# Two chained transformer layers: the decay levels, the memory keys and the hand-over between the layers reordered

## The reference, cut to what matters

```python
# first layer
xn   = rms_norm(x, norm1_g)
proj = xn @ w_in                                   # hq hf hi hgate gq gk gv glow ggate
o    = concat(hgrn2_mixer(...), gla_mixer(...))    # causal, decayed scores; per-head norm, silu gate
h    = x + o @ w_out
h    = h + peer_ffn(rms_norm(h, norm2_g), w_q, sub_keys, u, v)
x1   = rms_norm(h, norm_f_g)
# second layer
cols   = rms_norm(x1, norm_pre_2) @ w_in_2         # four branches and 4 x 1024 gate logits
mem_kv = rms_norm(mem_2, norm_mem_2) @ w_mem_kv_2  # memory keys (512 columns), values (512)
merged = sum_n sigmoid(gates[n]) * (ys[n] @ w_up_2[n])
out    = x1 + rms_norm(merged @ w_out_2, norm_post_2)
```

## Time and profile before

| | us |
|---|---|
| median of 3 runs | 1450.87 (1449.73 to 1451.43) |
| profiled execution, time | 1450.22 |
| profiled execution, span of its trace | 1448.4 |

### The profile page before, as it was taken

How to read it: one execution, slowest core, us unless ns; L and a number is a source line. 1 busy time by engine, 2 the same in 40 slices (tenths; PEclk the granted TensorE clock), 3 DMA queues, 4 the chain that set the end, 5 groups by cost and what they waited for, 6 DMA issues and landing times.

```text
span 1448.4 us, 22172 instructions
## 1 busy us (share of the span) xinstructions
PE 1415.0 (98%) x7922; PEld 1220.9 (84%) x7922; DVE 989.8 (68%) x1739; ACT 736.5 (51%) x1115; POOL 184.5 (13%) x176
## 2 busy tenths in 40 slices
PE   8998999999999999999999999999999999999998
PEld 8877888698788888888888888888889899888786
DVE  6577469899766666666666666666668564665565
ACT  5644321277555555555555555555555734465343
POOL 0062124699100000000000000000010100000000
PEclk9999999999999999999999999999999999999999
DMA  5442542211465555555555555555544432434442
GB/s 200 178 154 86 179 143 87 101 49 42 150 199 188 188 188 188 188 189 188 189 188 191 188 189 188 191 187 192 180 145 170 154 138 95 146 117 160 176 159 102
DMA packets 56342, 229.14 MB, mean 158 GB/s; under 512 B 6736, under 2 KB 7008, under 8 KB 47456
## 3 DMA queue, kind: packets, MB, share of 16 engines
q1 hardware_dynamic: 55824, 228.19, 46.4%
q10 hardware_dynamic: 464, 0.20, 0.0%
HBM read 226.27 MB, written 2.10 MB: 158 GB/s over the span
## 4 chain that ended last, share of the span: by engine, by line
PE 85%; DVE 7%; ACT 3%; DMA 2%; issue 1%; POOL 1%; ACTq 0%; DVEq 0%; POOLq 0%
PE ps L2265 22%; PE ps L2055 15%; PE ps L2254 13%; PE ps L2021 9%; PE ps L2252 8%; PE ps L2240 4%; PE ps L1978 3%; PE ps L2250 2%; PE ps L2217 2%; DVE lo L1386 2%; PE ps L2095 1%; ACT hi L889 1%; DMA raw<-in_v_t 1%; DMA raw<-in_pieces 1%; PE ps L2380 1%
## 5 line engine op out<-in xcount | busy, mean ns | idle before, releaser
L1595 DVE TENSOR_TENSOR lo<-raw,hi 128x1024 fp32r<-128x1024 f32 x234 | 286.0, 1222 | 61.9 <-ACT hi L1032 61.9
L2254 PE MATMUL ps<-x,hi 128*128 128x512 f32 x826 | 296.9, 398 | 0.0
L1032 ACT ACTIVATE hi<-raw 128x1024 fp32r<-128x1024 f32 x234 | 246.2, 1052 | 0.0
L2252 PE MATMUL ps<-x,lo 128*128 128x256 f32 x944 | 245.6, 281 | 0.0
L2055 PE MATMUL ps<-hi,x 128*128 128x512 f32 x704 | 227.7, 397 | 3.5 <-ACT big L1145 2.5
L1386 DVE TENSOR_TENSOR lo<-raw,hi 128x2048 fp32r<-128x2048 f32 x62 | 142.7, 2303 | 82.8 <-ACT hi L889 82.8
L2252 PEld LDWEIGHTS ps<-x,lo 128*128 128x128 f32 x944 | 178.5, 189 | 9.2
L2254 PEld LDWEIGHTS ps<-x,hi 128*128 128x128 f32 x826 | 155.2, 188 | 33.1
L1084 ACT ACTIVATE oi<-ps 128x256 f32<-128x256 f32 x118 | 45.2, 383 | 230.6 <-PE ps L2254 229.5
L2055 PEld LDWEIGHTS ps<-hi,x 128*128 128x128 f32 x704 | 133.9, 190 | 33.6 <-ACT big L1145 3.0
L2265 PE MATMUL ps<-hi,wh 128*128 128x512 f32 x488 | 151.7, 392 | 2.9 <-DVE wl L1605 2.6
(11 more groups left out here) (385 smaller groups left out, 2276.4 us busy)
## 6 DMA issues: line engine op xcount, KB each, us to landing
raw<-in_v_t SPq DMA_DIRECT2D x128, 512.0 KB, 3.5
raw<-in_u_t SPq DMA_DIRECT2D x126, 512.0 KB, 3.5
raw<-in_pieces SPq DMA_DIRECT2D x62, 1024.0 KB, 4.8
ring<-in_peer_w_q SPq DMA_DIRECT2D x4, 2048.0 KB, 8.0
big<-in_up SPq DMA_DIRECT2D x4, 2048.0 KB, 8.7
ring<-in_w_mem_kv SPq DMA_DIRECT2D x1, 2048.0 KB, 8.0
resid<-in_x SPq DMA_DIRECT2D x1, 1024.0 KB, 5.2
big<-in_mem SPq DMA_DIRECT2D x1, 1024.0 KB, 8.3
```

The lines of the kernel that those rows point to most:

```text
L1032: act.activation(hi[:, which, par], raw[:, which, par], ACT.Copy).then_inc(hi_done[which], 1)
L1595: dve.tensor_tensor(lo[:, which, par], raw[:, which, par], hi[:, which, par].bitcast(F32), ALU.subtract).then_inc(lo_done[which], 1)
L2252: pe.matmul(first, u_lo[:, par, c], xh[:, c], start=False, stop=False)
L2254: ins = pe.matmul(both, u_hi[:, par, c], x2[:, :, c], start=False, stop=(c == KC - 1))
```

## The change

No arithmetic of the results changes but the order in which two means are combined at the hand-over. The edits, by place:

1. Start: x comes as two transfers, the first piece as two halves right behind, with no wait for the parameters. The three memsets move behind the first splits. The softmax of the lower bounds moves behind the split of `hq1`. ScalarE and VectorE split half a piece, copy four chunks of x, and then the other halves.
2. Levels: `scores(0)` stands ahead of the gv pieces, `keep(0)` ahead of the split of `hgate0`, the first exponential ahead of the copies of gv. The split of `wo01` moves from level 4 to behind the first sum of squares. Levels 6 and 7 are kept as rectangles by plain copies. The scores across the tiles go to banks 6 and 7, and the first tile's product no longer waits for their copy. The four gate evacuations (Silu) come ahead of the last exponentials.
3. Memory: half of the transposes stand ahead of the last scores, half behind them. The keys' weights are loaded in two halves of 256 columns, to `gF` and `index_work` early and to `mixT` ahead of `wo11`. Eleven of the 48 steps stand around the transposes of the mixed rows, in place of the fill; `w_out` goes to banks 0, 1, 4 and 5.
4. Retrieval: 32, 44 and 4 in place of 24, 36 and 3.
5. Hand-over: the last key is written to `x2`, its V split comes ahead of its copy, `v_pass` signals each tile, `dnq0` is split in halves around the norm, the norm has one step of GpSimd for each tile and two of VectorE, the fill is 22 and 0 in place of 33 and 7.
6. Last gates: gate 21, 30 and 31 get banks 2/3, 0/1 and 2/3.

```diff
-CHUNKS_BEFORE_PICKS = 24
-CHUNKS_BEFORE_BUILD = 36
-BLOCKS_BEFORE_PICKS = 3
+CHUNKS_BEFORE_PICKS = 32
+CHUNKS_BEFORE_BUILD = 44
+BLOCKS_BEFORE_PICKS = 4
...
+        for n, h in ((2, 1), (3, 0), (3, 1)):
+            for k in range(NT):
+                g2_bank[f"gate{n}{h}{k}"] = 2 * (h % 2) + k
... SP
-            sp.dma_start(resid[:], t["x"].rearrange("b (n p) d -> p (b n) d", p=P)).then_inc(x_then_norm_f_loaded, 16)
+            for n, loaded in enumerate((x0_then_norm_f_loaded, x1_then_out_stored)):
+                sp.dma_start(resid[:, n], t["x"][0, n * P:(n + 1) * P, :]).then_inc(loaded, 16)
+            sp.dma_start(raw2[:, 0, 0:D], t["pieces"][0][:, 0:D]).then_inc(hq0a_then_mkv_moved, 16)
+            sp.dma_start(raw2[:, 0, D:2 * D], t["pieces"][0][:, D:2 * D]).then_inc(tile_loaded[0], 16)
...
-            sp.wait_ge(params_loaded, 64)
-            for k in range(NP1):
+            for k in range(1, NP1):
+                if loaded_pieces[k] == "wo11":
+                    sp.wait_ge(mem_T, 4)
+                    sp.wait_ge(cols_then_mem_loaded, 64)
+                    sp.dma_start(mixT, w_mem[:, :, T:2 * T]).then_inc(cols_then_mem_loaded, 16)
                 load_piece(k)
+                if loaded_pieces[k] == "wo01":
+                    sp.wait_ge(cum_done, 2 * NF)
+                    sp.dma_start(gF, w_mem[:, 0:NF, 0:T]).then_inc(cols_then_mem_loaded, 16)
+                    sp.dma_start(index_work.rearrange("p (c a) b -> p c (a b)", c=2), w_mem[:, NF:KC, 0:T]).then_inc(cols_then_mem_loaded, 16)
... VectorE
+            def keep_rectangles(n, m):
+                for k in range(4):
+                    tau, half = k // 2, k % 2
+                    dve.wait_ge(lvl_scores, 2 * n + tau + 1)
+                    dve.wait_ge(lvl_kept, 4 * (n - 1) + k + 1)
+                    for j in range(0, P, 2 * m):
+                        ins = dve.tensor_copy(own[j:j + m, tau, 4 * half:4 * half + 4, j + m:j + 2 * m],
+                                              ps[j:j + m, 4 + k, :].rearrange("p (h i) -> p h i", h=4)[:, :, j + m:j + 2 * m])
+                    ins.then_inc(lvl_kept, 1)
...
-                keep(l, masks[:, LEVELS if l == 0 else l - 1])
-                if 1 <= l <= 4:
+                elif l < LEVELS - 1:
+                    keep(l, masks[:, l - 1])
+                else:
+                    keep_rectangles(l, m // 2)
+                if 1 <= l <= 3:
                     piece_split_lo(next_piece(LEVEL_PIECES1[l - 1], 2))
... TensorE
             pe.wait_ge(fgate_done, 1)
             scores(0, qF, kF)
+            token_pieces("gv")
             for l in range(LEVELS):
...
+                if l == LEVELS - 1:
+                    pe.wait_ge(group_out, group_no["ggate1"] + 1)
+                    pe.wait_ge(mem_scaled, NT)
+                    transpose_memory(range(HALF))
...
-            pe.wait_ge(lvl_kept, 4 * LEVELS + 2)
+            transpose_memory(range(HALF, KC))
+            pe.wait_ge(lvl_kept, 4 * (LEVELS + 1))
...
-            pe.wait_ge(cross_out, 1)
-            pe.wait_ge(lvl_kept, 4 * (LEVELS + 1))
-            for n in range(NT):
+            for n in range(NT):
+                if n:
+                    pe.wait_ge(cross_out, 1)
...
+            memory(0, 9)
+            def mixed_ready(n):
+                if n:
+                    memory(9, 11)
+                pe.wait_ge(mixed_done, (n + 1) * HEADS1)
-            transpose_to_tiles(mixed, lambda n: pe.wait_ge(mixed_done, (n + 1) * HEADS1), (12, 4))
+            transpose_to_tiles(mixed, mixed_ready)
...
-            memory(20, MEM_STEPS)
+            memory(31, MEM_STEPS)
...
-            keep_busy(3, 33)
+            v_pass(NKEY, 1, last=True, key=last_key)
+            keep_busy(3, 22)
             pe.wait_ge(peer_out, 4)
-            transpose_by_tile(scaled2, lambda n: pe.wait_ge(scaled_done, 4 + n + 1), (0, 7, 3))
+            transpose_by_tile(scaled2, lambda n: pe.wait_ge(scaled_done, 4 + n + 1), (0, 0, 3))
... GpSimd
-                link(rsqrt(rstd_f[:, f], mean_f[:, f], sumsq_f[:, f], D, half))
...
-                pool.tensor_tensor(rstd_x[:, x], rstd_x[:, x], rstd_f[:, f], ALU.mult).then_inc(rstd_done, 1)
+                pool.wait_ge(hg_then_mean_done, NT + n + 1)
+                pool.tensor_tensor(rstd_x[:, one], mean_x[:, one], mhalf[:, 0:1], ALU.pow).then_inc(rstd_done, 1)
```

More of the change, by code:

```diff
@@ L1080, in second_key @@
             def second_key(n, v_loads, u_loads, par, last=False):
+                if last and par:
+                    act.wait_ge(v_mm, n - 2)
+                    split_hi(V, v_loads, par)
                 act.wait_ge(u_mm, n)
@@ L1473, in _ @@
                 part = resid[:, n, half * TILE:(half + 1) * TILE]
-                dve.tensor_tensor(part, part, ps[:, k, :], ALU.add).then_inc(h_done, 1)
+                dve.tensor_tensor(part, part, ps[:, 4 * half + n, :], ALU.add).then_inc(h_done, 1)
             for n in range(NT):
@@ L1604, in second_key @@
                 dve.wait_ge(wh_done, n)
-                dve.tensor_tensor(wl[:], act_j, wh[:].bitcast(F32), ALU.subtract).then_inc(wl_done, 1)
+                key_hi, key_lo = last_key if last and par else (wh[:], wl[:])
+                dve.tensor_tensor(key_lo, act_j, key_hi.bitcast(F32), ALU.subtract).then_inc(wl_done, 1)
                 if not last:
@@ L2168, in _ @@
                 if n == 0:
[L2169 to L2171 removed]
+                    memory(14, 16)
+            memory(16, 19)
             for k in range(2):
@@ L2266, in v_pass @@
                                             start=(first and k == 0), stop=(last and k == 2))
+                    if last and tau == 0:
+                        ins.then_inc(v_mm, 1)
                 ins.then_inc(v_mm, 1)
```

273 lines of the change are left out of this document (151 added, 122 removed).

## The result

The changed kernel takes 1431.47 us (median of four executions, 1430.41 to 1432.52), the kernel before 1450.53 in the same session: ratio 0.9868, interval 0.9851 to 0.9886, faster by 19 us or 1.3%. The profiled execution took 1430.41 with a span of 1428.7, against 1450.22 and 1448.4 before.

A forecast was written before the change was run, and what follows sets the result against it. TensorE was taken to bound 85% of the path, so cuts count only where it waits. -2.1 - 1.8 - 4.2 + 1.2 - 4.6 - 4.4 = -15.9 from 1450.22, plus 0.65 for the median, gives 1434.9 us; range 1429.5 to 1440.

The forecast's parts named there:

- the fall at the picks: Retrieval: TensorE's gap ahead of the picks grows to about 2.4 us and the granted clock falls behind it, +1.9 us.
- The case that had the largest chance: Whole kernel: all terms as summed, with the clock falling behind the gap at the picks, 1434.9 us; chance 0.47.
- the first rival: Picks: the clock holds behind the gap of about 2.4 us, 1.9 us less, 1433.0 us; chance 0.28.
- levels 0 to 3: Decay levels 0 to 3: reordered scores and keep(0) remove TensorE's wait of 1.77 us; -1.8 us, ends -1.2 and -2.5.
- start, up to hi: Start of the kernel: earlier loads and moved memsets bring the features forward; -2.1 us, ends -1.3 and -2.8.
- levels 4 to 7, mixed rows: Levels 4 to 7 and mixed rows: moved wo01 split, rectangles and unblocked first tile's product; -4.2 us, ends -2.0 and -5.5.
- retrieval: Retrieval: fewer half groups with a chunk, but a longer gap and clock fall at the picks; +1.2 us, ends -0.7 and +1.9.
- hand-over: Hand-over to the second layer: earlier last pass and earlier second scaling; net -4.6 us, ends -3.2 and -5.2.
- last gates: Last gates: other banks remove gate 21's wait of 2.54 us and 1.90 of slow clock; -4.4 us, ends -2.5 and -4.5.
- The late low part that was named for the worse end: Decay levels 0 to 3: the gate piece's low part comes late behind keep(0), leaving only -1.2 us.
- the first two items: Levels 4 to 7: wo01's split moved, -2.1 us; rectangles for masked copies, with memory transposes between scores, -1.0 us.
- the second rival: Levels: rectangles cost 0.64 each and the extra table load is exposed; stage gives 0.3, not 4.2, 1438.8 us; chance 0.09.

The follow-up runs named there:

- experiment 2: Changed kernel with 24, 36 and 3 chunks and blocks ahead, as before, in place of 32, 44 and 4: 1433.97 us.
- experiment 4: Changed kernel with the masked copies back in levels 6 and 7 in place of the rectangles: 1432.05 us.
- experiment 8: Changed kernel with the memset of kd moved from ahead of the forget gate to behind the low part of glow: 1430.80 us.
- experiment 11: Changed kernel with kd memset and wo01 low part moved, two fill matmuls behind glow, hi0 rounded before gqk1's copy, first fill 11 for 15: 1428.67 us.
- experiment 1: Kernel before with only the edit of the banks for gates 21, 30 and 31: 1445.45 us against 1450.0.
- experiment 5: Changed kernel with the low part of wo01 made in level 4 again: 1436.21 us.
- experiment 6: Changed kernel with the low part of wo01 made ahead of the first reduction, not between the two: 1430.92 us.
- experiment 9: Changed kernel with the hand-over norm back in GpSimd's seven small steps a tile, without VectorE's two steps: 1435.15 us.
- experiment 3: Changed kernel with 29, 40 and 3 chunks and blocks ahead in place of 32, 44 and 4: 1434.23 us.
- experiment 10: Changed kernel with the low part of dnq0 made whole ahead of the hand-over sums, nothing behind the second scaling: 1433.56 us.

## Why the prediction was right, point by point

Predicted were 1434.9 us and a range of 1429.5 to 1440.0; measured 1431.47. The sign and the order of the terms hold; the sum was 3.9 us short in the profiled execution (-19.8 against -15.9), and most of that is the clock: 1.9 for the fall at the picks, which was forecast and didn't come, and 1.6 for the one at hi, which was not in the sum. The case that had the largest chance was the one with the fall at the picks. The median is nearer to the first rival, 1433.0, and 1.5 below it. So the number lies in the range although the branch taken for the clock was wrong: both misses went the same way and the range had room for them, while the other terms are off by 1.1 (levels 0 to 3) or 0.7 at most. That the profiled execution has no fall at hi is luck.

| term | predicted | measured |
|---|---|---|
| start, up to hi | -2.1 | -1.4 |
| clock at hi | none | -1.6 |
| levels 0 to 3 | -1.8 | -2.9 |
| levels 4 to 7, mixed rows | -4.2 | -3.8 |
| retrieval | +1.2 | -0.9 |
| hand-over | -4.6 | -4.8 |
| last gates | -4.4 | -4.4 |

- **Start.** The features begin at 14.17, 14.0 to 14.2 was said: the fill was what binds next. The wait for the low part of `gqk1` behind the memset was in the text, at 0.3 to 0.8, and is 0.55. I put it against the sum but took -2.1, nearer the end without it. The 0.4 for a first tile no longer paced by VectorE didn't show: from the features to hi it takes 40.51 us and took 39.86, the 0.55 and 0.1 more. That the first fill ends at 8.86 "whatever comes" is wrong: with the moment at which the pace changes, the transposes behind it begin between 8.70 and 9.89, at 9.15 in the profiled execution. Against experiments 2 and 4, where the pace changes as early as in the trace of before, the start gives 56.06 - 54.21 = 1.85. Experiment 8 removes the wait. That the fill could be cut, too, I read over: its end was named as the bound, and 0.9 us lay there (experiment 11).
- **Clock at hi.** The prediction had no such term. The trace of before has a stretch at 0.50 behind the gap of 0.44, and I looked for the clock only at gaps of over a microsecond. Its absence in the profiled execution of the changed kernel is no merit of the change: experiments 1, 5, 6, 8 and 9 have it.
- **Levels 0 to 3.** The gap of 1.77 went as said, and two more of 0.16 and 0.20 ahead of the gv pieces, which I had left out. The term is 5.81 - 1.38 - 1.57 = 2.9 at level 1 against 2.1 of gaps. The rest lies beside them: three pieces of 24 matmuls take 16.46 us without a gap, 5.49 each, and took 5.60 to 5.74 each next to one, the gap not counted. The late low part that was named for the worse end does occur in some executions: in experiments 3, 4 and 10 TensorE waits 0.39 to 0.40 us ahead of the first gate piece.
- **Levels 4 to 7.** The scores across the tiles start 8.95 us earlier (137.84 and 128.89), 3.1 beyond level 1's shift, as the first two items said (-2.1 and -1.0). The first tile's product gives 1.2 more (1.1 said). Then the mixed rows lose 0.6, to the step that GpSimd made beside VectorE's subtraction; the sum had nothing for it, and experiment 6 returns it. The rectangles' price, taken from copies of the same size, was near: 2.41 and 1.60 measured, 2.1 and 1.6 estimated. The split between the items was wrong: I gave the split of `wo01` 2.1, and experiment 5 gives it 2.2 of gap and 2.8 of clock (1.6 in the kernel before), which the memory transposes, 2 x 1.09 between the scores, then take back in part. ScalarE's table was reloaded in cover, as said.
- **Retrieval.** Here the step failed. Forecast was a gap of 2.4 and a fall of the clock; the rival, 1433.0, had the gap and no fall. It was neither: the gap is 1.15, and the clock held. My sum was 4.7 us less of memory steps and 3.5 more of chunks. But the 32 chunks took 15.43 us (255.10 to 270.53) and the 24 before 10.79 (269.39 to 280.18), 4.64 more: TensorE waits 0.78 for the load of the fourth block and 0.15 for an earlier one, and the last 0.2 stand in no gap. I had counted the chunks as work alone and not asked when their data come; in the kernel before, 24 chunks never waited. What the clock does behind a gap of 2.4 remains open; at 2.68 it fell (experiment 3).
- **Hand-over.** -1.1 for the last pass against -1.1, -3.6 for the rest against -3.5 net. The shorter chain on GpSimd and the halves of `dnq0` both stand on the path (experiments 9 and 10), and hide 0.8 of each other.
- **Last gates.** Exact, and experiment 1 shows it alone.
- The rivals: the levels did shrink, the banks did what they say, and the loop kept its 5.55 us. The price of the second rival was too low: its 3.9 are the 2.6 of level 6 and the 1.3 of the table, while the 1.0 that the sum had credited at the same place would have gone too. Two neighbouring keys in the changed kernel's chain in order of time, answering:

```profile
1029.13 2.74 PE ps L2343 x12
...
1034.68 2.74 PE ps L2343 x12
```

## What to carry to other kernels

A gap of TensorE is priced twice, once as waiting and once by the clock behind it: here all gaps of 2.5 us and more inside the work cost another 1.4 to 2.8 us, those of 0.9 to 1.8 nothing, so the first thing to ask of an edit is whether a gap passes from the one group to the other. Two short gaps close together have to be priced as a pair. The matmuls at the start of the program run at the slower pace, so a fill that is last there is longer than its count says. When work is moved ahead to fill a gap, count also when its data land. When a large two-input operation of VectorE is moved into a quiet place, look who on GpSimd works there; the better place is the one in which VectorE waits for a third engine and GpSimd has nothing to do.

## What the runs showed of the hardware that was not expected

- A small step of GpSimd can run as long as VectorE's operation beside it: 2.17 us for 8 numbers a partition, starting 0.17 behind VectorE's subtraction of 128x2048 and ending 0.06 after it, 0.20 without it (experiment 6); 1.27 and 1.43 in place of 0.19 and 0.55 at the hand-over beside the products of 128x1024 (experiment 9). Not every operation does this: the same step took 0.20 at 139.06 in the changed kernel, beside the mixed rows, which VectorE reads from PSUM. The rows show the coincidence, not the resource that is shared.
- The first matmuls of every run start 0.21 us apart and later ones of the same shape 0.11. The moment of the change differs by up to 2.7 us between executions, and where a fill is last, half of it or so shows in the time (0.5 us for 1.0, 1.2 for 2.5).
- Two gaps of 0.46 and 0.44 us around thin matmuls are followed by a clock of 0.50 in some executions and not in others, 1.6 us apart.
- Copies from PSUM took 0.30 us for 32 partitions of 128 elements and 0.40 for 64 of 256. The steps of the mixed rows, 128 partitions of 128 elements, took 0.27, so more partitions didn't make a row of 128 slower.
